# Higher powers of the state-space tables made on GpSimd, and the projection's second weight tile requested after the first has landed

## The reference

```python
# first_block
mod = jax.nn.silu(c) @ ada_w[i] + ada_b[i]
shift, scale, gate = jnp.split(mod[:, None, :], 3, axis=-1)
h = x * (1.0 + scale) + shift
pz = h @ w_in
# s5_discretise
abar = jnp.exp(lam * dt)
bbar = ((abar - 1.0) / lam)[..., None] * bmat
```

## Time and profile before

| | |
|---|---|
| time before, median of 3 runs | 1594.21 us (1588.92 to 1595.09) |
| the profiled execution | 1591.13 us, span 1589.3 us |
| TensorE busy | 1521.7 us (96%) |
| VectorE busy | 982.8 us (62%) |
| ScalarE busy | 791.1 us (50%) |
| GpSimd busy | 649.0 us (41%) |
| HBM traffic | 202 GB/s over the span |

### The profile page before, as it was taken

How to read it: one execution, slowest core, us unless ns; L and a number is a source line. 1 busy time by engine, 2 the same in 40 slices (tenths; PEclk the granted TensorE clock), 3 DMA queues, 4 the chain that set the end, 5 groups by cost and what they waited for, 6 DMA issues and landing times. The chain is left out here.

```text
span 1589.3 us, 28594 instructions
## 1 busy us (share of the span) xinstructions
PE 1521.7 (96%) x11520; PEld 1307.2 (82%) x11520; DVE 982.8 (62%) x1368; ACT 791.1 (50%) x1072; POOL 649.0 (41%) x497
## 2 busy tenths in 40 slices
PE   5999999999899899998999999999999999999998
PEld 3777788688788688888889987879999877799997
DVE  7567422689645449669566557746666665466665
ACT  5312222566412677787554336745544463555542
POOL 0689799499499892479311116020000101200000
PEclk9999999999999999999999999999999999999999
DMA  9989977665444678989785446335445232455440
GB/s 381 344 293 302 334 262 252 214 206 187 164 147 165 205 247 235 279 254 277 196 311 193 181 160 220 114 131 220 180 179 217 90 143 101 159 189 231 165 182 29
DMA packets 120593, 331.33 MB, mean 208 GB/s; under 512 B 33800, under 2 KB 73480, under 8 KB 104224
## 3 DMA queue, kind: packets, MB, share of 16 engines
q1 hardware_dynamic: 117300, 289.79, 53.4%
q10 hardware_dynamic: 3180, 39.95, 6.8%
HBM read 283.49 MB, written 37.83 MB: 202 GB/s over the span
## 5 line engine op out<-in xcount | busy, mean ns | idle before, releaser
L3547 PE MATMUL ffn_ps<-ffn_x_lead,w_lead 128*128 128x256 f32 x672 | 188.4, 280 | 1.1 <-DVE w_rest L3626 1.1
L3547 PE MATMUL ffn_ps<-ffn_x_lead,w_rest 128*128 128x256 f32 x672 | 188.6, 281 | 0.0
L3547 PE MATMUL ffn_ps<-ffn_x_rest,w_lead 128*128 128x256 f32 x672 | 188.4, 280 | 0.0
L419 POOL TENSOR_TENSOR w_rest<-resident_ring,w_lead 128x2048 fp32r<-128x2048 f32 x7 | 32.1, 4591 | 379.6 <-ACTq L3488 187.6
L3626 DVE TENSOR_TENSOR w_rest<-resident_ring,w_lead 128x2048 fp32r<-128x2048 f32 x42 | 96.1, 2292 | 83.8 <-ACT w_lead L3591 83.8
L3547 PEld LDWEIGHTS ffn_ps<-ffn_x_lead,w_lead 128*128 128x128 f32 x672 | 126.1, 188 | 2.2 <-issue 1.5
L3547 PEld LDWEIGHTS ffn_ps<-ffn_x_rest,w_lead 128*128 128x128 f32 x672 | 126.4, 188 | 0.7
L3547 PEld LDWEIGHTS ffn_ps<-ffn_x_lead,w_rest 128*128 128x128 f32 x672 | 126.3, 188 | 0.0
L285 DVE TENSOR_TENSOR w_rest<-resident_ring,w_lead 128x2048 fp32r<-128x2048 f32 x33 | 78.2, 2373 | 62.5 <-ACT w_lead L279 62.2
L3591 ACT ACTIVATE w_lead<-resident_ring 128x2048 fp32r<-128x2048 f32 x42 | 80.1, 1913 | 50.7 <-PE ffn_ps L3547 50.6
L285 DVE TENSOR_TENSOR qkvz_w_rest<-resident_ring,qkvz_w_lead 128x2048 fp32r<-128x2048 f32 x20 | 54.1, 2706 | 82.3 <-ACT qkvz_w_lead L279 82.3
(11 more groups left out here) (621 smaller groups left out, 4625.8 us busy)
## 6 DMA issues: line engine op xcount, KB each, us to landing
resident_ring<-in_ffn_gu SPq DMA_DIRECT2D x22, 2048.0 KB, 9.1
ffn_wd<-in_ffn_down SPq DMA_DIRECT2D x22, 1024.0 KB, 4.9
xc<-s_q_scratch SPq DMA_DIRECT2D x128, 128.0 KB, 3.6
resident_ring<-in_ada_w ACTq DMA_DIRECT2D x8, 2048.0 KB, 8.7
resident_x<-in_s_bT SPq DMA_DIRECT2D x64, 256.0 KB, 4.4
resident_ring<-in_attn_w_in ACTq DMA_DIRECT2D x8, 2048.0 KB, 8.9
s_W_scratch<-resident_x SPq DMA_DIRECT2D x64, 256.0 KB, 4.1
resident_ring<-in_s_w SPq DMA_DIRECT2D x32, 512.0 KB, 6.2
```

The source lines that it names most:

```text
L419: self.core.nc.gpsimd.tensor_tensor(self.slots[1][0], self._raw(r), self.slots[0][0].bitcast(F32), ALU.subtract).then_inc(self.rest_made, 1)
L3547: last = nc.tensor.matmul(ps[s][f][:, m, :], w_part[w][m][:, k, f * P:(f + 1) * P], x_part[x][:, k, :], start=(k, w, x) == (0, 0, 0), stop ...
```

## The change

The four squarings leave VectorE's chain and become GpSimd's stream in phase `ada`, with temporaries of their own (`l1`, `l2`) and a semaphore of their own (`level_steps`). GpSimd waits for three increments of `powers` (so for all of `pw`) and gives the fourth itself. VectorE goes from `pw` straight to `qst`. Apart from that, SyncE waits for the landing of the first `attn_w_in` tile before it requests the second.

```diff
@@ phase ada, SyncE
                 for s in range(2):
                     sp.wait_ge(mm_done, NT - 2 + s)
+                    if s:
+                        sp.wait_ge(core.landed[0], 16 * (landed_before[0] + 2))
                     core.load(sp, s, d["attn_w_in"][s])
                 tab_q_store(sp)
+
+            @block.gpsimd
+            def _(pool):
+                tab_pool(pool)
@@ s5_tables
+    l1, l2 = ph.sb("tab_l1", [P, 1, 2, P]), ph.sb("tab_l2", [P, 1, 2, P])
@@ s5_tables, on_vector
         for n in (1, 2, 4):
             product([(pw[:, n:2 * n], slice(0, P))], pw[:, n - 1, 0, :], pw[:, n - 1, 1, :], pw[:, 0:n], n)
             dve.sem_inc(powers, 1)
-        for l in range(LEVELS - 1):
-            of = pw[:, CH - 1] if l == 0 else sq[:, l - 1]
-            product([(sq[:, l:l + 1], slice(0, P))], of[:, 0, :], of[:, 1, :], of.unsqueeze(1), 1)
-        dve.sem_inc(powers, 1)
@@ s5_tables
+    def on_gpsimd(pool):
+        chain, g = Chain(pool, level_steps), nc.gpsimd
+        wide = lambda m: m.unsqueeze(1).unsqueeze(1).to_broadcast([P, 1, 2, P])
+        pool.wait_ge(powers, 3)
+        for l in range(LEVELS - 1):
+            of = pw[:, CH - 1] if l == 0 else sq[:, l - 1]
+            src = of.unsqueeze(1)
+            g.tensor_tensor(l1[:], wide(of[:, 0, :]), src, ALU.mult)
+            chain.run(g.tensor_tensor(l2[:], wide(of[:, 1, :]), src[:, :, ::-1, :], ALU.mult))
+            for c, op in ((0, ALU.subtract), (1, ALU.add)):
+                last = g.tensor_tensor(sq[:, l:l + 1, c, :], l1[:, :, c, :], l2[:, :, c, :], op)
+            chain.run(last)
+        pool.sem_inc(powers, 1)
```

More of the change, by code:

```diff
@@ L596, in modulation @@
         tiles = [core.tile(0), core.tile(1), third]
-        (tab_loads, tab_scalar, tab_empty, tab_tensor, tab_vector, tab_stores, tab_q_store) = s5_tables(core, ph, z, kn)
+        (tab_loads, tab_scalar, tab_empty, tab_tensor, tab_vector, tab_pool, tab_stores, tab_q_store) = s5_tables(core, ph, z, kn)
         late.store_tables = tab_stores
@@ L1451, in s5_tables @@
     banks = [ph.ps(f"tab_ps{s}", [P, 4, P]) for s in range(TB)]
-    names = "loads steps to_act from_act powers staged turned emptied".split()
-    loads, steps, to_act, from_act, powers, staged, turned, emptied = [ph.sem("tab_" + n) for n in names]
+    names = "loads steps level_steps to_act from_act powers staged turned emptied".split()
+    loads, steps, level_steps, to_act, from_act, powers, staged, turned, emptied = [ph.sem("tab_" + n) for n in names]
     halves = (slice(0, SS), slice(SS, P))
@@ L1592, in q_store_on_sync @@
         sp.dma_start(d["s5_q"], qst).then_inc(core.q_stored, 16)
-    return loads_on_sync, on_scalar, empty_on_scalar, on_tensor, on_vector, stores_on_sync, q_store_on_sync
+    return loads_on_sync, on_scalar, empty_on_scalar, on_tensor, on_vector, on_gpsimd, stores_on_sync, q_store_on_sync
 class ScaledInput:
```

## The result

| | kernel before | changed kernel |
|---|---|---|
| median of the timed runs | 1592.73 us (9 runs) | 1598.15 us (9 runs) |
| ratio, 95% interval | | 1.0052 (1.0035 to 1.0069) |
| profiled execution, span | 1589.3 us | 1599.3 us |
| GpSimd's or VectorE's last squaring ends | 27.70 us | 36.63 us |
| projection's stream starts on TensorE | 35.36 us | 41.68 us |

The change makes the kernel slower, by 5.4 us between these medians. Their quotient is 1.0034; the ratio in the table is the recorded estimate from the same runs and lies higher, so it should be read with its interval. The view by windows has the same split as the earlier trace rows, cut again 2 to 3 us behind the first product's start; columns are length, TensorE busy time, granted clock, DMA share and GB/s.

What follows compares the result with a forecast made beforehand. The first weight tile's landing, then TensorE's steady work, was taken to bound the kernel. A mean of 1592.3 us plus 6.6 for the ramp and 0 for the held-back tile gave 1598.9, stated as 1598.5; range 1592 to 1603.

Steps and rivals of the forecast that it cites:

- What bounds the kernel before: Start of the projection: the first weight tile's landing at 36.28 us sets ScalarE's copy, so faster VectorE brings nothing.
- Price of a level: One squaring level on undisturbed GpSimd in phase `ada`: 2.45 us, four levels 9.8 us.
- Loss beside VectorE: GpSimd squaring beside VectorE's `qst` loses 85% of 6.8 us, 5.8 us; squarings end at 38.0, bounds 32.3 to 39.1.
- From the squarings to the projection: TensorE's transposes and small products at half clock, then the barrier: 4.6 us, projection starting at 42.6.
- Ramp: From the projection's start to its first product: `h_lead` at 44.75, 6.6 us later; first product at 48.4.
- The tile: SyncE's held-back second tile request: costs nothing beside the moved squarings, 1.4 us alone; landing by 45.
- part 1: Phase `ada`: the squarings moved to GpSimd, ending at 38.0 us, 10.3 us later than before.
- The sum: Whole kernel: 6.6 us for the later entry plus 0 for the held-back tile, giving 1598.5 us.
- SyncE last: At the barrier: GpSimd ends by 32.4, SyncE's wait decides, costing 1.4 us, 1593.7 us; chance 0.14.
- GpSimd slow by itself: Squarings in phase `ada`: four levels cost 14.5 us on GpSimd, ending at 42.8, 1603.3 us; chance 0.12.
- an earlier first tile: First weight tile lands up to 5 us sooner without the second behind it; at best 1593.3 us; chance 0.04.
- a barrier that does not bind: Barrier before the projection: the change is lost in TensorE's slack, 1592 us; chance 0.04, shared with anything below 1591.

Runs made afterwards that it cites:

- e7: Kernel before with the four squarings left out and made nowhere (sq zero); ratio 1.0004.
- e8: Kernel before with the first projection tile requested as two 1 MB DMAs, ScalarE's first copy waiting for the first half only; ratio 0.9985, median 1588.47 us.
- e5: Changed kernel without VectorE's product for `qst`, so VectorE is idle during most of GpSimd's squarings; ratio 1.0007.
- e6: Changed kernel with GpSimd starting its squarings only after VectorE finished `qst`; executed once, no ratio, first product at 49.12 us.
- e1: Changed kernel with the second tile requested as before, so only the squarings move to GpSimd; ratio 1.0046, median 1595.42 us.
- e3: Changed kernel with 36 instead of 38 blocks of S5 input weights made on GpSimd during the projection; ratio 1.0032.
- e11: Changed kernel timed once more, unaltered; ratio 1.0035, median 1595.63 us.
- e12: Changed kernel with 36 instead of 38 S5 weight blocks during the projection, timed a second time; ratio 1.0026, median 1594.14 us.
- e2: Kernel before with only the second tile's request held back, squarings still on VectorE; ratio 1.0015, median 1592.74 us.
- e4: Kernel before with 36 instead of 38 S5 weight blocks during the projection; ratio 1.0000.

## Why the prediction was right

**What bounds the kernel before.** The landing of the first tile, not VectorE, sets the first product, as predicted. e7 shows it by removing the squarings (copy at 36.43, product at 41.93), e8 by moving the landing (product 0.8 earlier, then held by the barrier).

**Price of a level.** Forecast 2.45 us, measured 2.31 (e5, and the last two levels of the changed kernel). The pair of 128x128 operations costs 0.86, so 0.43 each where I took 0.45, and the 128x256 one has a pitch of 0.63 instead of the 0.70 read from rows 8.

**Loss beside VectorE.** Forecast 5.8 of 6.8 us. Measured: 14.16 us from 22.47 to 36.63 for what takes 9.24 alone (e5), a loss of 4.9, and VectorE lost 2.6 itself (22.48 to 31.71 for 6.64). The end came at 36.6 instead of 38.0, inside the bounds of 32.3 to 39.1: 0.6 us of the difference are the cheaper levels and 0.9 the smaller loss. Of VectorE's 2.6, 1.0 fell on the four copies, which have one input each and of which the prediction had said nothing. The rule of the Trainium skill (SBUF — State Buffer, "Who interferes with whom") says that the second to issue is blocked until the first is through. The trace agrees where it is clearest: the two operations merged in the row at 23.90 end at 26.22 and 28.41, each 0.3 us after one of VectorE's multiplications (25.90 and 28.10). As a sum it was too strict: taken over all of `qst` it gave 39.1, or 22.47 + 9.24 + 6.64 = 38.35 with the measured terms, and one after the other e6 ends at 38.48, the change at 36.63, so 28% of VectorE's work did overlap. Some 0.4 us of that is VectorE's copies, beside which GpSimd's rows kept their length; where the rest lies is not shown.

**From the squarings to the projection.** Forecast 4.6 us, measured 5.05 (36.63 to 41.68). At the clock's lower level the ten transposes and eight products took 3.90 us (36.74 to 40.64) against 2.07 before (28.17 to 30.24), 1.8 more where I took 1.3. This error and that of the squarings' end offset each other in part: the start was forecast at 42.6 and came at 41.68.

**Ramp.** `h_lead` 43.84 against a forecast 44.75, first product 47.27 against 48.4: 5.5 us later than before where I said 6.6. The step between the two took 3.43 us, against 3.68 before. e1, e3, e11 and e12 repeat it at 47.05 to 47.27.

**The tile.** Forecast free beside part 1 and 1.4 alone. e1 and e2 show both (47.05 with part 1 alone; 43.18, +1.4, with part 2 alone). It landed at 44.9, forecast 45, and ScalarE did not wait for it. That holding it back gives the first tile nothing shows in the first tile's landings: 36.2 to 36.4 in the profiles with the second request right behind a whole first tile, 36.0 to 36.4 in those without. But "one tile comes after the other" was too simple a reason: without the second tile hardly any data moved in the last 2 us before the landing.

**The sum.** That 1598.5 lies beside the measured 1598.15 is in part luck: the entry costs 5.5 us, not 6.6, and the runs of one kernel spread by 10 us. By the entry alone the ratio would be 1.0035, which is what the repeated run, e1 (1.0046) and the pair e3 and e12 (1.0032 and 1.0026) surround. The first measurement's 1.0052 lies over the 0.5% that I gave a chance of 0.19 (the quotient of its medians, 1.0034, does not), and its profile has 4.5 us more behind the first product, 3.3 of them by the end of the projection. I had also put what a measurement can tell from no change at about 0.5%; the intervals came out at 0.17 to 0.2% to either side, so a cost of 5.5 us was told apart from none each time. "Nothing behind it gives that back" was right; that something behind it could add to it I had not looked for, although the trace of before showed GpSimd's chain of blocks ending only 1.9 us ahead of TensorE. I had read only who waits, and nobody waited for that chain yet.

**Rivals.** SyncE last is what e5 and e2 show once GpSimd is quick or not there; GpSimd slow by itself is out (e5); an earlier first tile is out (e1, e2); a barrier that does not bind is out (e2).

Open: how much the end of the projection costs on average. Runs of one kernel spread over 10 us (the S5 stage alone lasts between 288.2 and 295.3 us in the profiles taken), and pairs differing by it alone (e11 and e12, e4 and before) agree within their intervals of about 0.2%.

No version here beats the kernel before beyond doubt: e8 is 0.15% under it with an interval that ends at 1.0002.

## What to carry to other kernels

Before moving work off an engine that is last at a barrier, look one step on: if the step behind the barrier starts with a DMA's landing, the barrier may have slack, and then a shorter chain in front of it is worth nothing until the landing moves (here the transposes came 3.1 us earlier, and nothing was won). Work moved from VectorE to GpSimd beside VectorE's own two-input operations has to be priced as mostly serial (28% overlapped here), and whatever is queued behind the moved work pays its delay, here TensorE's transposes, at a granted clock of 0.50 after the pause. A request that waits for a landing holds up its whole queue, the end of its block included.

## What the runs showed of the hardware that I had not expected

VectorE and GpSimd don't share evenly. GpSimd's two 128x128 operations took 4.52 us beside two VectorE multiplications of 128x1792 that ran at 2.01 and 2.27 (2.02 alone), while later four shorter VectorE operations took 3.57 instead of 2.23 and GpSimd's rows 1.4 to 1.8 times their time. Over the whole stretch GpSimd lost 4.9 us and VectorE 2.6.

The granted clock stayed at 0.50 for long after a pause: in the changed kernel TensorE worked again from 36.74, with one more pause of 1.05 us, and the clock rose only at about 45.6 us (46.5 in e11, 44.5 in e12). What it did in between were transposes and other small products, of 128x128 and 128x2. Before, after a pause of 5.1 us, the clock was 0.50 as well and rose at about 39.4, 4.0 us after the projection's first transpose.
